# GpSimd waits for VectorE's eight low parts at four norms of a transformer kernel

## The reference

```
for l in range(2):
    u = rms_norm(h, attn_norm[l])
    proj = u @ w_in[l]                       # 1024 x 7424
    ...three kinds of attention, gates, w_out...
    h = h + merged @ w_out[l]
    m = rms_norm(h, mlp_norm[l]) @ w_mlp_in[l]   # 1024 x 4096
    h = h + square(relu(m)) @ w_mlp_out[l]
```

## Time and profile before

| what | us |
|---|---|
| median of 3 runs | 1844.46 |
| lowest and highest of them | 1844.4, 1844.8 |
| the profiled execution | 1844.82 |
| its span in the trace | 1843.0 |

### The profile page before, as it was taken

How to read it: one execution, slowest core, us unless ns; L and a number is a source line. 1 busy time by engine, 2 the same in 40 slices (tenths; PEclk the granted TensorE clock), 3 DMA queues, 4 the chain that set the end, 5 groups by cost and what they waited for, 6 DMA issues and landing times.

```text
span 1843.0 us, 30281 instructions
## 1 busy us (share of the span) xinstructions
PE 1813.7 (98%) x11948; PEld 1619.7 (88%) x11948; DVE 1261.1 (68%) x1662; ACT 516.6 (28%) x842; POOL 515.3 (28%) x574
## 2 busy tenths in 40 slices
PE   7999999999999999999999999999999999999999
PEld 4777777888989888888899999988899999898888
DVE  6657564336267887788598966886666886788665
ACT  3000001013123412322135544432112555442210
POOL 2211211211144014444340002364434000326442
PEclk9999999999999999999999999999999999999999
DMA  9347774221333424455544433445545433345552
GB/s 373 134 157 298 264 269 152 101 91 69 115 138 130 179 76 159 160 182 206 183 171 166 145 138 116 182 171 195 185 180 183 161 140 135 137 161 183 186 202 91
DMA packets 45197, 307.07 MB, mean 167 GB/s; under 512 B 5536, under 2 KB 6048, under 8 KB 8736
## 3 DMA queue, kind: packets, MB, share of 16 engines
q1 hardware_dynamic: 41200, 293.71, 43.7%
q10 hardware_dynamic: 3888, 11.78, 1.8%
HBM read 302.33 MB, written 3.15 MB: 166 GB/s over the span
## 4 chain that ended last, share of the span: by engine, by line
PE 88%; DVE 7%; issue 3%; ACT 1%; DMA 1%; DVEq 0%; ACTq 0%; POOL 0%; POOLq 0%
PE ps L2194 44%; PE ps L2242 12%; PE ps L2282 7%; PE ps L2221 6%; PE ps L2288 4%; DVE wlo L776 4%; PE ps L2869 1%; PE ps L2264 1%; PE ps L2268 1%; PE ps L2265 1%; PE ps L2442 1%; PE ps L2893 1%; PE ps L2879 1%; DVE xparts L862 1%; PE ps L2744 1%
## 5 line engine op out<-in xcount | busy, mean ns | idle before, releaser
L776 DVE TENSOR_TENSOR wlo<-landing,whi 128x1024 fp32r<-128x1024 f32 x482 | 610.4, 1301 | 233.3 <-PE ps L2242 74.9
L2194 PE MATMUL ps<-xparts,whi 128*128 128x256 f32 (+1 forms) x3232 | 495.6, 311 | 3.8 <-ACT xparts L1723 2.1
L2194 PEld LDWEIGHTS ps<-xparts,whi 128*128 128x128 f32 x3232 | 443.7, 192 | 43.1 <-issue 8.0
L691 POOL TENSOR_TENSOR whi<-landing,ones 128x16 fp32r<-128x16 f32 x184 | 89.9, 489 | 1289.4 <-PE ps L2194 717.6
L2194 PE MATMUL ps<-xparts,wlo 128*128 128x256 f32 (+1 forms) x2368 | 346.7, 299 | 2.0 <-DVE wlo L776 2.0
L2194 PEld LDWEIGHTS ps<-xparts,wlo 128*128 128x128 f32 x2368 | 320.0, 191 | 20.3 <-DVE wlo L776 3.0
L693 POOL TENSOR_SCALAR whi<-landing 128x1008 fp32r<-128x1008 f32 x184 | 210.5, 1144 | 0.0
L694 POOL TENSOR_SCALAR whi<-landing 128x1024 fp32r<-128x1024 f32 x184 | 208.8, 1135 | 0.0
L2221 PE MATMUL ps<-xparts,whi 128*128 128x512 f32 x752 | 180.1, 392 | 0.0
L2221 PEld LDWEIGHTS ps<-xparts,whi 128*128 128x128 f32 x752 | 138.4, 188 | 27.0
L2242 PE MATMUL ps<-xparts,whi 128*128 128x256 f32 (+1 forms) x960 | 155.0, 319 | 0.0
(11 more groups left out here) (307 smaller groups left out, 2005.3 us busy)
## 6 DMA issues: line engine op xcount, KB each, us to landing
landing<-in_stream SPq DMA_DIRECT2D x248, 1024.0 KB, 4.8
ws<-in_stream SPq DMA_DIRECT2D x25, 1024.0 KB, 4.9
big<-in_stream SPq DMA_DIRECT2D x4, 1024.0 KB, 5.9
spectra<-big ACTq DMA_DIRECT2D x8, 256.0 KB, 4.3
ws<-spectra ACTq DMA_DIRECT2D x2, 1024.0 KB, 4.8
ws<-in_tabs ACTq DMA_DIRECT2D x1, 1280.0 KB, 7.0
h<-in_xT ACTq DMA_DIRECT2D x1, 1024.0 KB, 5.4
ws<-in_ctxT SPq DMA_DIRECT2D x1, 1024.0 KB, 7.2
```

Of the source, the lines that this page charges most:

```text
L691: pool.tensor_tensor(hi[:, 0:FIRST], panel[:, 0:FIRST], ones[:, 0:FIRST], ALU.mult)
L776: ins = v.tensor_tensor(wlo[:, s % 2, c], panel[:, c], whi[:, s % 2, c].bitcast(F32), ALU.subtract)
L2194: ins = mm(out, a, b, start=first and opens and k == ks[0], stop=last and k == ks[-1], skip_group_check=True)
```

## The change

At each of the four norms GpSimd stops before panel 1 until `norm_lo` shows that VectorE has made the low parts of all eight chunks. Panel 0's high part is made before that wait (by GpSimd at A and C, by ScalarE at B and D). What each instruction computes is the same; no instruction of another engine moves. As `highs` is now called for shorter ranges, some panels are written out one by one instead of in the loop.

```diff
             def highs(begin, end):
-                whole = -(-begin // UNROLL)
+                whole, last = -(-begin // UNROLL), end // UNROLL
+                if last - whole < 2:
+                    for g in range(begin, end):
+                        high(g, g % SLOTS, g // SLOTS)
+                    return
                 for g in range(begin, whole * UNROLL):
                     high(g, g % SLOTS, g // SLOTS)
-                with pool.Fori(whole, end // UNROLL) as i:
+                with pool.Fori(whole, last) as i:
                     for j in range(UNROLL):
                         high(i * UNROLL + j, j, i)
-                for g in range(end - end % UNROLL, end):
+                for g in range(last * UNROLL, end):
                     high(g, g % SLOTS, g // SLOTS)
+
+            def behind_norm(begin, end, j):
+                highs(begin, end)
+                pool.wait_ge(norm_lo, (5 + j) * KD + KD)
+                return end
...
             for l in range(LAYERS):
                 for i in range(PER_LAYER):
+                    if i in (1, O_MIN + 1):
+                        begin = behind_norm(begin, layer_panel(l, i)[0], 2 * l + (i > 1))
                     if i in ACT_HIGH:
```

## The result

| what | before, us | after, us |
|---|---|---|
| median (8 runs each) | 1844.9 | 1850.66 |
| lowest and highest | 1844.4, 1846.58 | 1848.89, 1852.75 |
| the profiled execution | 1844.82 | 1850.76 |
| its span | 1843.0 | 1849.0 |

The ratio is 1.0032, with a 95% interval of 1.0022 to 1.0041. The change makes the kernel 5.8 us slower. The forecast was 1845.2 us, its range ended at 1848.0, and so it was wrong: a loss of 0.7 us was forecast, and 5.8 came.

The account below looks back on a forecast made before the run. TensorE, busy 98%, bounds the kernel, so only its waits count. A +1.2, B +0.15, C -0.8 and D +0.15 sum to +0.7 us, giving 1845.2 us; range 1841.8 to 1848.0.

Parts of the forecast that it names:

- the gain on offer: At the norms, L862 running alone gains TensorE 0.78 us at A and 1.1 each at B, C, D: 4.1 us.
- Panel 1 starts at T + 3.3: Behind each norm, T being the last L862's end: TensorE starts panel 1 about 0.2 us late, awaiting GpSimd's high part.
- Only at A the term: Norm A: the last of the L862 ends 0.78 us earlier once they run alone.
- GpSimd's panel 2, held off as before until VectorE's pause: Norm C: GpSimd's panel 2 comes about 0.9 us later and may cost 0.1; gain kept 0.8 us.
- `fold` ends 0.85 later, in time: Norms B and D: TensorE does not wait for `fold`; the loss is 0.15 us each, at panel 3.
- nobody waits: Norm C: `fold` ends at 1393.35 and TensorE comes for it at 1394.0, so the late VectorE delays nobody.
- the shift of 1.2: Norm A: VectorE, without reserve, is 1.2 us later and this arrives whole; loss 1.2 us, bounds 0.2 and 2.0.
- Rival 3: Behind the norms, GpSimd gets in after a single VectorE instruction, between panel 1's low halves: +4.0 us, 1848.5; chance 0.04.
- Rival 2: VectorE's chain behind the norm becomes the bound at A, B and D: up to +3.2 us, 1847.7; chance 0.17.
- Rivals 1 and 4: 1: the gain stays, the later chain bends, 1842.0 us, chance 0.22. 4: low parts already done, wait does nothing, 0.01.

Follow-up runs that it names:

- last kernel: Against the kernel before: ScalarE instead of GpSimd makes panel 1's high part at all four norms, ahead of ScalarE's last two squares; 1841.57 us, ratio 0.9982.
- only the program split: The changed kernel without the new wait, GpSimd's program only split differently (more panels written out, shorter loops); 1845.16 us, ratio 1.0004.
- `fold` was left alone: The changed kernel plus a GpSimd wait for the end of `fold` before panel 2 (panel 3 at A); 1848.72 us, ratio 1.0018.
- the kernel where VectorE waits for both halves: The changed kernel, VectorE beginning panel 1's low part at the norms only when both halves of its high part are there; 1856.5 us, ratio 1.0062.
- first ScalarE kernel: Against the kernel before: ScalarE makes panel 1's high part, behind the whole norm at B and D, ahead of its last squares at A and C; 1841.56 us.

## Why the prediction was wrong

**Right: the gain on offer.** L862 alone again, TensorE's waits for it gone, 1.1 us at B, C and D. Panel 1 starts at T + 3.3, VectorE's pair takes 3.2 and ends at T + 5.4. The last kernel shows the gain pure. Only at A the term was too large: the last L862 was to end 0.78 us earlier and ended 0.35 earlier (5.24 us behind the first instead of 5.59), because undisturbed it had to wait for ScalarE's high part:

```profile
926.33 0.89 DVE L873 SCALAR_TENSOR_TENSOR xparts<-h,gains,xparts 128x256 fp32r<-128x256 f32 x2 [0.34 <-ACT xparts L1697]
```

**The step that failed** is half a sentence on norm C: "GpSimd's panel 2, held off as before until VectorE's pause". I carried L691's 3.40 us in the earlier trace rows over to a place where VectorE no longer ran in one piece. In the changed kernel L691 waits 1.20, `fold` is stretched from 3.18 to 4.86 us, and on top of the late start, which the prediction had (0.92 us at D, 0.85 forecast), that makes TensorE wait: at B and D "`fold` ends 0.85 later, in time" (at D it ends 2.6 us later, counted from the first low part: 4.45 + 10.25 against 5.59 + 6.51, and TensorE waits 1.18), at C "nobody waits" (TensorE waits 1.00), at A the shift of 1.2. Nor was the 3.40 as firm as its three places in the trace of before make it look: with only the program split, it is 1.07 at B and 1.04 at C.

**By norm.** C was to gain 0.8 and lost 0.31. B and D were to lose 0.15 each at panel 3 and lost 0.95 and 0.89, most of it ahead of panel 2. A was to lose 1.2, at most 2.0, and lost 3.86: 2.61 by the sums and 1.5 by the clock, less some 0.4 that came back. Ahead of the sums the two `fold`s start 1.56 us later, counted from the first low part, and take 1.65 longer (8.08 us in all, from T + 9.54 to T + 17.62, instead of 6.43).

**The rivals.** Rival 3 had the mechanism, L691 in after a single instruction, and nearly its price, +4.0, against 4.5 measured without the clock (6.01 - 1.5). In part that is luck: it has -0.5 at C, where +0.31 came, and 1.15 each at B and D, where 0.95 and 0.89 came, and it prices a delay of VectorE by one L693 (1.03), where the rows show `fold` 1.68 longer. I gave it 0.04, on the ground that L691 had been passed over at three ends of L776. These were two ends of L776 and one of L877, as L691 came during the second of the three L776, and they counted as three observations what was one situation. Two things spoke for more: the trace of before has a case of the other kind, L691 of panel 3 at D (at B and C too), which waited one instruction only,

```profile
1670.00 1.18 POOL L691 TENSOR_TENSOR whi<-landing,ones 128x16 fp32r<-128x16 f32 x1
```

while the L776 that it met had itself just been held up by GpSimd's L694 of panel 2. And there is the Trainium skill's rule (SBUF — State Buffer, Who interferes with whom) that the shared pair is an exclusive lock, which whoever issues first gets for the whole instruction. Read as a lock of one instruction and not of several, it would have given what came. In this case that reading agrees with the changed kernel's 1.20 us and not with the 3.40 of before. Rival 2, the late chain of VectorE to L1605, did not decide in the changed kernel; it did when `fold` was left alone, with 1.5 us of waiting at each of B and D. Rivals 1 and 4 fell.

**Left out altogether** was TensorE's clock. Neither the sum nor the range had a term for what a wait of over two microseconds does to the matmuls behind it, and it is a quarter of the loss (1.5 of 6.0).

## What to carry to other kernels

A row that shows an engine held off by another is one outcome, even if three places of the trace repeat it; before it is carried over, price the other outcome too, and look for it in a second trace of the same instructions. If a helper engine disturbs a critical stretch, taking work off it (here to ScalarE, which had the time) keeps the gain, while putting the same work off by a wait moves the contention onto the next stretch, together with the panels that queue behind it. And a wait of TensorE's should be priced with the matmuls that follow it: 2.62 us of idle time came with 1.5 us more.

## What the runs showed of the hardware

**A GpSimd instruction can be passed over, or not.** L691, 0.22 us when free, came to panel 2 while VectorE ran without a stop at B, C and D of before and of the last kernel, and waited through four VectorE instructions (3.40 to 3.41 us, and 3.27 to 3.34). In the same situation it was in after one instruction at B and C of the kernel with only the program split (1.07 and 1.04 us). Where VectorE had just stood still ahead of panel 1's pair, for 0.25 to 2.21 us, it was not passed over in any trace: it was in after one instruction (1.20, 1.27 and 1.18 us), or at once if it came first (0.23). Once in, GpSimd was never passed over: from norm A on no L693 or L694 of any trace took more than 2.07 us, against 1.03 free, in turns with VectorE. What decides between the two was not found.

**TensorE's clock after an idle time.** Behind 2.62 us of waiting at A the granted clock over five microseconds was 0.66 and 32 matmuls took 5.67 us instead of 4.17; with 20 matmuls in that gap, and 0.25 us of waiting left, it stayed at 1.00. It fell behind the wait at A in each of the four traces where that wait was 2.60 to 2.95 us. Behind the waits at the norms of 0.97 to 1.54 us it stayed at 1.00. Behind 1.94 us at C and 2.06 us at D, in the kernel where VectorE waits for both halves, it fell (the 32 matmuls at C took 5.66 us):

```profile
1405.00:1410.00 5.00, 5.00 (x33) 5.00 (x33) 3.16 (x5) 0.19 (x1) 0.32 (x2) 0.71 0.59 211
1685.00:1690.00 5.00, 5.00 (x22) 4.21 (x21) 4.82 (x6) 1.11 (x2) 0.94 (x2) 0.72 0.64 210
```

At B of the same kernel, behind 2.08 us, the clock did not fall. And behind a wait of 2.07 us near 732 us, which every trace has, it fell in ten of the twelve traces: in the trace of before it is 0.66 from 735 to 740 us, in the traces of `fold` left alone and of the first ScalarE kernel 1.00. So the length of the wait alone does not decide it.
